# A decoder layer on one core: block 1's output products, norm and first queries placed ahead of blocks 2 and 3, units and branch products over 93 rows, a fourth weight buffer

## The reference

```
z      = x @ W_in            # 9 sections of 1024 columns: q, forget, i, out-gate | conv B, C, h | gate_a, gate_b
o_A    = gated linear recurrence over q, forget, i (8 heads), RMS norm, times silu(out-gate)
o_B    = B * causal_depthwise_conv3(C * h)
mix    = (sigmoid(gate_a) * (o_A @ W_a) + sigmoid(gate_b) * (o_B @ W_b)) @ W_out
x      = LayerNorm(ALPHA * x + mix)
# PEER: per token, 8 heads
qh     = x @ w_q                                    # 8 heads x 2 halves x 128
s1, i1 = top16(qh[:, h, 0] @ keys[h, 0].T);  s2, i2 = top16(qh[:, h, 1] @ keys[h, 1].T)
eidx   = the best 16 of the 256 sums s1 + s2, as i1 * 128 + i2;  g = softmax of these 16
peer   = sum over h, k of g * gelu(u[eidx] . x) * v[eidx]      # u, v: 16384 rows of 1024
x      = LayerNorm(ALPHA * x + peer)
x      = x + sigmoid(x @ W_pg) * (p @ W_pp)
```

## Time and profile before

| | |
|---|---|
| three runs, us | 1784.62 (median), 1783.69, 1786.54 |
| the profiled execution's own time, us | 1783.85 |
| its span, first to last instruction, us | 1781.9 |
| PE busy | 1572.8 us (88%) |
| DVE busy | 1321.1 us (74%) |
| ACT busy | 778.3 us (44%) |
| POOL busy | 497.4 us (28%) |
| moved by DMA | 655.40 MB, of which 536.90 MB by the gathers |
| mean granted TensorE clock | 0.984 |

### The profile page before, as it was taken

How to read it: one execution, slowest core, us unless ns; L and a number is a source line. 1 busy time by engine, 2 the same in 40 slices (tenths; PEclk the granted TensorE clock), 3 DMA queues, 4 the chain that set the end, 5 groups by cost and what they waited for, 6 DMA issues and landing times. The chain is left out here.

```text
span 1781.9 us, 16998 instructions
## 1 busy us (share of the span) xinstructions
PE 1572.8 (88%) x5000; PEld 874.4 (49%) x5000; DVE 1321.1 (74%) x2804; ACT 778.3 (44%) x1937; POOL 497.4 (28%) x528
## 2 busy tenths in 40 slices
PE   8999999999999997989888668788898878787778
PEld 7888888766655575544344223333333323222224
DVE  4454588599888999678878886886666687766666
ACT  6567695422222224343334334444444443444453
POOL 0000000122222232324333443333333333333331
PEclk9999999999999999999999999999999999999999
DMA  5113289799999999999999999999999999999994
GB/s 205 70 70 141 94 317 402 281 421 421 397 419 421 422 406 404 424 417 421 421 415 415 421 421 422 420 422 421 421 421 422 419 408 422 422 419 421 422 410 179
DMA packets 94933, 655.40 MB, mean 368 GB/s; under 512 B 10368, under 2 KB 14208, under 8 KB 17152
## 3 DMA queue, kind: packets, MB, share of 16 engines
q0 software_dynamic: 73728, 536.90, 72.8%
q1 hardware_dynamic: 20832, 116.97, 16.7%
q10 hardware_dynamic: 288, 0.52, 0.1%
HBM read 652.26 MB, written 2.10 MB: 367 GB/s over the span
## 5 line engine op out<-in xcount | busy, mean ns | idle before, releaser
L2111 PE MATMUL psum<-uv,diag 128*128 128x512 f32 x1424 | 707.3, 627 | 193.3 <-ACT diag L991 189.9
L720 POOL DMA_INDIRECT uv<-in_pk_uv,idx x512 | 495.0, 967 | 1249.6 <-PE psum L2111 563.9
L1596 DVE CUSTOM_DVE_ANT_0 uv<-uv,psum 128x1024 f32<-128x1024 f32 x512 | 622.9, 1217 | 295.1 <-DMA uv<-in_pk_uv,idx 288.0
L2111 PEld LDWEIGHTS psum<-uv,diag 128*128 128x128 f32 x1424 | 257.7, 194 | 613.2 <-ACT diag L991 389.7
L979 ACT ACTIVATE gelu<-dots 128x1 f32<-128x1 f32 x512 | 103.5, 202 | 764.1 <-DVE dots L1596 761.9
L2011 PE MATMUL psum<-xT,raw 128*128 128x384 f32 x640 | 208.4, 486 | 0.0
L1609 DVE SCALAR_TENSOR_TENSOR oT<-uv,coef,oT 128x1024 f32<-128x1024 f32 x151 | 193.3, 1280 | 4.2 <-ACT coef L983 4.2
L2011 PEld LDWEIGHTS psum<-xT,raw 128*128 128x128 f32 x640 | 120.7, 190 | 81.7
L983 ACT ACTIVATE coef<-gelu,weight 128x1 f32<-128x1 f32 x512 | 150.8, 295 | 16.6
L991 ACT ACTIVATE diag<-ident,coef 128x128 f32<-128x128 f32 x356 | 143.0, 402 | 11.6
L1847 PE MATMUL psum<-xTh,w_hi 128*128 128x512 f32 x248 | 98.6, 398 | 0.0
(11 more groups left out here) (284 smaller groups left out, 1722.5 us busy)
## 6 DMA issues: line engine op xcount, KB each, us to landing
raw<-in_w_in SPq DMA_DIRECT2D x32, 1024.0 KB, 8.9
raw_a<-in_w_a SPq DMA_DIRECT2D x12, 1024.0 KB, 4.8
raw<-in_pk_w_q SPq DMA_DIRECT2D x10, 1024.0 KB, 9.5
raw_y<-in_w_in SPq DMA_DIRECT2D x8, 1024.0 KB, 6.8
raw<-in_w_branch_a SPq DMA_DIRECT2D x8, 1024.0 KB, 7.7
uv<-in_pk_uv,idx POOLq DMA_INDIRECT x512, 14.6
raw<-in_w_out SPq DMA_DIRECT2D x6, 1024.0 KB, 9.6
raw_w<-in_pk_w_q SPq DMA_DIRECT2D x6, 1024.0 KB, 9.5
```

Source lines behind the costliest of these rows:

```text
L720: pool.indirect_dma_start(row_uv(r)[:], None, pk_uv, bass.IndirectOffsetOnAxis(idx[:, i % 2, j:j + 1], 0)).then_inc(row_loaded(r)[0], 16)
L1596: V.tensor_tensor_reduce(u, u, x_cur[:], 1.0, 0.0, ALU.mult, ALU.add, dots[:, r % 32:r % 32 + 1]).then_inc(dot_done, 1)
L2111: last = T.matmul(B[i][:], diag[:, n % DR, :], row_uv(r)[:, D + i * 512:D + (i + 1) * 512], start=(r in FIRST), stop=last_of_block, skip_g ...
```

## The change

The order of the work beside the rows is rewritten; nothing of what is computed changes.

- Units take rows 0 to 67 (MERGE0 = 68), branch products 68 to 92.
- Output products: the four chunks of block 1 at rows 94 to 98, then blocks 2 and 3 at rows 99 to 112. Norms at rows 101, 115, 117; turns at 104, 118, 120.
- Heads 0 and 1 (SPLIT = 2) are queried for block 1 alone, at rows 106 to 108 and 111 to 113, and for blocks 2 and 3 together at 122 to 125 and 128 to 131; heads 2 to 7 for all three blocks from row 134.
- A thirteenth slot, number 12, in the columns of blocks 2 and 3 of the scores' first half; the loads from unit load 2 to the output chunks go through four slots (RING). Unit load 2 goes to slot 12 and waits for nothing; each later load waits for the load four before it, not three.
- SHARED holds block 0's rows up to 112 and no others of block 0. MERGE_R is 105 (before 91), QUERY_R 212 (211).
- SP loads w_gate behind the fourth of the new query loads and w_ple behind head 1's second query.
- In the final part, block 0 is turned at row 149, its gate products are at 152 to 167, its projection at 169 to 172.

```diff
+            if i == 12:
+                return scores[:, 0, :, 2 * P:]
...
+        SPLIT = 2
+        MERGE0 = 68
...
-        UNIT_ROW += [[(UNIT_MM * n + i) * 58 // (UNIT_MM * (len(UNITS) - EARLY)) for i in range(UNIT_MM)]
+        UNIT_ROW += [[(UNIT_MM * n + i) * MERGE0 // (UNIT_MM * (len(UNITS) - EARLY)) for i in range(UNIT_MM)]
...
-        MERGE_ROW = [58 + n * 23 // 128 for n in range(16 * KT)]
-        OUT_ROW = [83 + n * 11 // 96 for n in range(4 * (TB - 1) * KT)]
-        NORM_ROW = [None] + [OUT_ROW[-1] + 1 + 2 * b for b in range(1, TB)]
+        MERGE_ROW = [MERGE0 + n * 25 // 128 for n in range(16 * KT)]
+        OUT0 = MERGE_ROW[-1] + 2
+        OUTS = [(c, 1) for c in range(4)] + [(c, b) for c in range(4) for b in range(2, TB)]
+        OUT_ROW = [OUT0 + n * 5 // 32 for n in range(4 * KT)]
+        OUT_ROW += [OUT0 + 5 + n * 14 // 64 for n in range(4 * (TB - 2) * KT)]
+        NORM_ROW = [None, OUT0 + 7] + [OUT_ROW[-1] + 3 + 2 * b for b in range(TB - 2)]
...
+        LATER = [(1, h) for h in range(SPLIT)] + [(2, h) for h in range(SPLIT)] + [(1, h) for h in range(SPLIT, PKH)]
+        QUERY0 = {(1, 0): (TURN_ROW[1] + 2, 3), (1, 1): (TURN_ROW[1] + 7, 3), (2, 0): (TURN_ROW[3] + 2, 4),
+                  (2, 1): (TURN_ROW[3] + 8, 4), (1, 2): (TURN_ROW[3] + 14, 6), (1, 3): (TURN_ROW[3] + 22, 7)}
+        QUERY0.update({(1, h): (123 + 14 * (h - 2), 9) for h in range(4, PKH)})
...
-                if r <= OUT_ROW[-1] + 3:
-                    return True
-                return r % 3 == 1 and 106 <= r <= 120
+                return r <= OUT_ROW[-1]
...
-        MERGE_R, QUERY_R = BLOCK_ROWS - 2 - 5 * (UV + 1), QUERY_ROW[-1][-1] + 11
+        MERGE_R, QUERY_R = BLOCK_ROWS - 2 - 3 * (UV + 1), QUERY_ROW[1, PKH - 1][-1] + 11
...
-        FIN_TURN = 5
-        FIN_GATE = [8 + n for n in range(2 * KT)]
+        FIN_TURN = [21] + [5] * (TB - 1)
+        FIN_GATE = [[t + 3 + n for n in range(2 * KT)] for t in FIN_TURN]
...
-        LOADS += [(("unit", n), n - 2 if n < 4 else (n - 2) % 3) for n in range(2, len(UNITS) // 2)]
-        LOADS += [(("merge", m), m % 3) for m in range(8)]
-        LOADS += [(("out", c), (c + 2) % 3) for c in range(4)]
-        LOADS += [(("query", 1, h), h % 2) for h in range(PKH)]
+        RING = (0, 1, 2, 12)
+        LOADS += [(("unit", n), 12 if n == 2 else RING[(n - 3) % 4]) for n in range(2, len(UNITS) // 2)]
+        LOADS += [(("merge", m), RING[(m + 1) % 4]) for m in range(8)]
+        LOADS += [(("out", c), RING[(c + 1) % 4]) for c in range(4)]
+        LOADS += [(("query", 1, h), (1, 2, 0)[h] if h < 3 else h % 2) for h in range(PKH)]
...
             fetch(pk_w_q[2], "query", 0, 2)
-            sp.wait_ge(t_done, USE["unit", 1] + 1)
             unit_fetch(2)
             for h in (3, 4, 5):
                 sp.wait_ge(t_done, USE["query", 0, h - 3, 1] + 1)
                 fetch(pk_w_q[h], "query", 0, h)
+            sp.wait_ge(t_done, USE["unit", 1] + 1)
+            unit_fetch(3)
             sp.wait_ge(t_done, USE["unit", 3] + 1)
-            unit_fetch(3)
+            unit_fetch(4)
...
-            query_fetch(0)
-            query_fetch(1)
-            sp.wait_ge(t_done, chunk_end(11))
-            sp.dma_start(w_ple[:], ple_w_proj).then_inc(ple_in, 16)
-
+            for h in range(4):
+                query_fetch(h)
             sp.wait_ge(x1_done, TB)
             sp.dma_start(w_gate[:], ple_w_gate).then_inc(gate_in, 16)
-            query_fetch(2)
-            query_fetch(3)
+            sp.wait_ge(t_done, query_end(2, 1))
+            sp.dma_start(w_ple[:], ple_w_proj).then_inc(ple_in, 16)
             load_p(0)
```

More of the change, by code:

```diff
@@ L229, in build @@
         first_in = [sem(f"first_in{j}") for j in range(4)]
-        raw_in = [sem(f"raw_in{i}") for i in range(12)]
+        raw_in = [sem(f"raw_in{i}") for i in range(13)]
         consts = sem("consts")
@@ L373, in row_previous @@
             return max((q for q in range(r) if UV_SLOT[q] == UV_SLOT[r]), default=None)
-        FIN_TURN = 5
-        FIN_GATE = [8 + n for n in range(2 * KT)]
-        FIN_P = [FIN_GATE[-1] + 2 + n for n in range(4)]
+        FIN_TURN = [21] + [5] * (TB - 1)
+        FIN_GATE = [[t + 3 + n for n in range(2 * KT)] for t in FIN_TURN]
+        FIN_P = [[rows[-1] + 2 + n for n in range(4)] for rows in FIN_GATE]
         P_BANK = (6, 4)
@@ L433, in blocks, with asked, asked_with @@
             return range(*PIECES[pc])
+        def asked(pc, h):
+            if pc == 1:
+                return range(1, 2 if h < SPLIT else TB)
+            return range(0, 1) if pc == 0 else range(2, TB)
+        def asked_with(i):
+            b, h = divmod(i, PKH)
+            return 0 if b == 0 else 2 if b > 1 and h < SPLIT else 1
         USES, BANK = [], []
@@ L474, in build @@
                     use(UNIT_BANK[n % 4], "unit", n)
[L475 to L482, removed]
+        for n in range(16):
+            use(4 + (n + 2) % 4, "merge", 1, n // 4, n % 4)
+        for r in range(OUT_ROW[0], SCORE_ROW[1, PKH - 1] + 1):
+            for n, (c, b) in enumerate(OUTS):
+                if r == OUT_ROW[KT * n + KT - 1]:
+                    use(4 + (n + 2) % 4 if b == 1 else (0, 1, 6, 7)[n % 4], "out", 1, c, b)
+            for b in range(1, TB):
+                if r == TURN_ROW[b]:
+                    for kh in range(2):
+                        use((4 if b == 1 else 6) + kh, "turn", 1, b, kh)
+            for q in LATER:
+                for a in range(2):
+                    if r == QUERY_ROW[q][KT * a + KT - 1]:
+                        use(4 + a, "query", *q, a)
+                if r == SCORE_ROW[q]:
+                    for a in range(2):
+                        use(4 + a, "query", *q, 2 + a)
         USE = {name: n for n, name in enumerate(USES)}
@@ L529, in chunk_end, with query_end @@
             return USE["out", 1, m - 8, TB - 1] + 1
+        def query_end(pc, h):
+            return USE["query", pc, h, 1] + 1
         @block.sync
@@ L1007, in tail_row @@
                         turn_out(1, b)
-                for h in range(PKH):
+                for q in LATER:
                     for a in range(2):
[L1010 to L1013, removed]
+                        if r == QUERY_ROW[q][KT * a + KT - 1] + 1:
+                            query_out(*q, [a])
+                    if r == SCORE_ROW[q] + 1:
+                        query_out(*q, [2, 3])
             def x2_turn_out(b):
@@ L1453, in search @@
                 if k == 0:
-                    dve.wait_ge(*t_reader(USE["query", min(i // PKH, 1), i % PKH, 3]))
+                    dve.wait_ge(*t_reader(USE["query", asked_with(i), i % PKH, 3]))
                     for a in range(2):
@@ L1741, in tail_row @@
                         merge(1, n // 4, n % 4)
-                for n in range(4 * (TB - 1)):
+                for n, (c, b) in enumerate(OUTS):
                     if r == OUT_ROW[KT * n + KT - 1] + 3:
-                        residual(1, n // (TB - 1), 1 + n % (TB - 1))
+                        residual(1, c, b)
                 for b in range(1, TB):
@@ L2062, in query @@
             def query(pc, h, a, ks=range(KT)):
-                bs = blocks(pc)
-                t = slice(bs[0] * P, (bs[-1] + 1) * P)
+                bs = asked(pc, h)
                 n = P * len(bs)
-                w = slot(SLOT["query", pc, h])
-                turned = x1T0 if pc == 0 else oT[:, :, P:]
+                name = ("query", min(pc, 1), h)
+                w = slot(SLOT[name])
+                turned = x1T0 if pc == 0 else oT[:, :, bs[0] * P:(bs[-1] + 1) * P]
                 r = USE["query", pc, h, a]
@@ L2071, in query @@
                     if k == 0:
-                        pe.wait_ge(*loaded("query", pc, h))
+                        pe.wait_ge(*loaded(*name))
                         if h == 0 and pc > 0:
-                            pe.wait_ge(*t_reader(USE["turn", pc, bs[-1], 1]))
+                            pe.wait_ge(*t_reader(USE["turn", 1, bs[-1], 1]))
                         t_free(r)
@@ L2091, in score @@
                     for i in range(len(bs)):
-                        last = T.matmul(B[bank(r)][:, i * P:(i + 1) * P], qhT[pc][:, a, i * P:(i + 1) * P],
+                        last = T.matmul(B[bank(r)][:, i * P:(i + 1) * P], qhT[pc > 0][:, a, (at + i) * P:(at + i + 1) * P],
                                         keysT[:, 2 * h + a, :], start=True, stop=True, skip_group_check=True)
@@ L2201, in tail_row @@
                         turn_x(1, b)
-                for h in range(PKH):
-                    for n, t in enumerate(QUERY_ROW[h]):
+                for q in LATER:
+                    for n, t in enumerate(QUERY_ROW[q]):
                         if r == t:
-                            query(1, h, n // KT, [n % KT])
-                    if r == SCORE_ROW[h]:
-                        score(1, h)
+                            query(*q, n // KT, [n % KT])
+                    if r == SCORE_ROW[q]:
+                        score(*q)
```

59 lines of the change are left out of this document (29 added, 30 removed).

## The result

The changed kernel takes 1803.99 us (median, 1802.99 to 1808.61), the kernel before 1785.53 us (1783.69 to 1786.54) beside it: ratio 1.0106, 95% interval 1.0093 to 1.0119, so 18.9 us slower (0.0106 of 1784.6, as all ratios below are turned into us; the medians are 18.5 apart). The forecast was 1786.1, with 1792.0 as its upper end. The profiled execution is the slowest of the changed kernel's: own time 1808.61 us, span 1806.6, against 1783.85 and 1781.9 before. Its 24.7 us more are to be explained in the trace. Some 3.3 us of them belong to this one execution and not to the change: it issues its first gather at 340.00 us, while all ten other profiled runs of this document issue theirs at 335.85 to 337.24.

The account below looks back on a forecast made before the run. The DMA pipe, saturated by gathers from about 340 to 1750 us, was taken as the bound. Terms -1.1 - 0.8 + 2.4 + 0 + 1.0 = +1.5 us gave 1785.3, with 0.8 for the median 1786.1; range 1781.0 to 1792.0.

Parts of the forecast that it names:

- The load of w_gate moves from row 108 to about 127, w_ple behind row 131: SP's later weight loads: same bytes, wanted at rows 152 and 169, so cost 0.
- block 0's gate matmuls to rows 152 to 167: Block 0's final part, moved to later rows: same work, cost 0.
- The spread: Units and branch products over 93 rows: TensorE gets cover, DMA idle at 450 and 640 us is won, -1.1 us.
- +11 sums: Block 0's rows 0 to 112 summed on VectorE, 113 in place of 102: 13 us more on it, +1.0 us.
- ring: Fourth weight buffer, slot 12: early unit load -0.8 us, 1 KB packets +2.4 us, slower landings 0.
- early load: Unit load 2 moves into the idle pipe before the first gather: -0.8 us, bounds 0 and 2.5.
- The packets: Slot-12 loads in 1 KB runs, 21 us each: 0.35 us lost a load, +2.4 us for seven, bounds 0 and 4.
- The full stretch of VectorE: Rows 94 to 112, VectorE and pipe about even: idle at 700:720 us stays and as much again, +1.0 us, bounds 0 and 6.
- Slot-12 loads come late: Rival: out load 2 or 3 lands after VectorE needs it at row 101, +4 to +10 us, 1791; chance 0.15.
- VectorE becomes the bound in rows 85 to 112: Rival: 13 us more VectorE work there and one buffer less leave DMA idle, +3 to +6 us, 1790.5; chance 0.15.

Follow-up runs that it names:

- e1: The changed kernel with the ln2_bias load issued ahead of the wait for head 1's second query and of w_ple: 1792.83 us, ratio 1.0046.
- e2: e1 with the w_gate load also moved ahead of head 3's queries: 1787.47 us, ratio 1.0015.
- e4: The kernel before with only the ln2_bias load moved, behind head 4's queries: 1793.68 us, ratio 1.0053.
- e5: e2 with block 0's projection moved later, to rows 174 to 177: 1784.34 us, ratio 1.0003.
- e8: The kernel before with block 0's final part 16 rows later (gate 152 to 167, projection 169 to 172): 1787.97 us, ratio 1.0022.
- e3: The kernel before with only slot 12 and the early unit load added: 1785.45 us, ratio 1.0003.
- e6: e5 with the sums of rows 115, 118, 121 and 124 on VectorE in place of TensorE: 1786.48 us, ratio 1.0014.
- e7: e5 with units back in rows 0 to 57 and branch products in 58 to 80: 1796.93 us, ratio 1.0075.
- e9: e5 without the four-slot ring and early unit load; slot 12 keeps one load, head 3's queries get another slot: 1784.09 us, ratio 0.9998.

## Why the prediction was wrong

In order of size, against +18.9:

- *"The load of w_gate moves from row 108 to about 127, w_ple behind row 131 ...: same bytes, wanted at 152 and 169. Cost 0"*. **This is the step that failed.** It looked up when w_gate and w_ple are wanted and never named what is queued behind them: ln2_bias, 0.5 MB, wanted at row 132. Moving w_ple's wait ahead of it costs 10.7 us (e1), w_gate's late place another 5.5 (e2), together 16.2. e4 gives the same kind of loss, 9.5, by the bias's order alone. Nor did it ask what the pipe does at the place that w_gate leaves: at 755:780 it falls to 345 GB/s in the changed kernel and stays at 425 with w_gate there (e2), which is some 2.5 of the 5.5 us.
- *"block 0's gate matmuls to rows 152 to 167"*, also at cost 0: the projection follows them to 169 to 172, where TensorE is full with head 5's queries. 2.1 us by e5, 3.9 by e8. I had asked only whether the work was the same, not what TensorE does in the new rows.
- The spread, +11 sums, ring and early load, which I had at +1.5 together, measure +0.5 (-1.1 to +2.1, e5). That the sum comes so near is in part luck, as each term was off and the errors cancel; the next four points go by the table of leads, in which two traces differ by about 1 us without a cause.
- The early load: I had -0.8, since I took the gathers' start to leave idle what the load had won. The whole 1.05 MB counts: the pipe is 1.9 to 3.0 us ahead at 345 in e1, e2, e3, e5, e6 and e7. The hole is partly filled (at 320:340 the kernel before moves 171 GB/s, e5 229), and the first gather leaves at 336.61 in e5 (336.66 in the earlier trace rows).
- The packets: the pace was right, 20 us of transfer and landings at 25.1 to 31.9 us, median 26.0, in e5 (21 and 25 in the sum), and small packets rose by 22400 - 14208 = 8192. The price was not: 3.5 us, near the upper bound of 4, not 2.4. I had averaged two windows of some 2.5 us each, too short to show the rate. I had also worked out a price, 1.4 us as an estimate, from the fixed cost of about 3 cycles a packet that the Trainium skill ("DMA: Bandwidth & Descriptors", Why small descriptors are slow) states; the traces show more than twice that, and the measurement decides.
- The spread: I had -1.1. e9, without ring and early load, gains 3.4 us from 345 to 690. I had read the idle pipe by its share; by the rate, against 421 GB/s, has 1.5 us at 450:460 and 1.8 at 640:660; both dips are gone (417 and 422 GB/s after). At 660:670 of the kernel after the share is 1.03 and the rate 403 GB/s; at 710:720 before it is 0.95 and 382, 6% by the share and 9% by the rate. GB/s is the measure of the pipe.
- The full stretch of VectorE behind it: I had +1.0; e5 loses 1.9 us from 690 to 760. The dip at 700 to 720 stayed, as foretold (400 and 361 GB/s against 392 and 382).
- *"Slot-12 loads come late"*: not in the change. Loads to the old slots do get slower (raw<-in_w_in 11.7 us to landing in place of 8.9), yet VectorE is busy 59.64 of 60 us at 640:700. The rival's mechanism is real all the same, as e7 shows (6.6 us).
- *"VectorE becomes the bound in rows 85 to 112"*: 1.9 us in e5, under the 3 to 6 of the rival, and 3.9 in the trace of the changed kernel, 690 to 760 us in both; e6 pays for four sums more. Which part of the 3.9 is the missing w_gate load of 755:780 is not shown.

The chance of a slower kernel was put at 0.30, and no rival named the wait that came. The mechanism that all of it goes through, a pipe that is paid for whenever it stands empty, was right; I didn't apply it to the loads of the norm.

## What to carry to other kernels

When an issue with a wait moves in a queue that runs in order, list every later issue of that queue with its own due time, the smallest ones too: half a megabyte, 13 us late to leave, cost 10.7 us, the place of a load of 4.2 MB 5.5 us. Work moved "to later rows at the same cost" needs a look at how full its engine is in these rows and at who reads the result in order. A large load is also filler: it costs least where the engines that free the buffers are full and the pipe would idle. And where the DMA pipe is the bound, compare the bytes moved up to fixed times: by the end alone the spread, the early load and the small packets looked like nothing, while they moved the pipe by 3.4, 2.5 and 3.5 us.

## What the runs showed of the hardware

```profile
DMA packets 1775, 7.37 MB, mean 410 GB/s; under 512 B 99, under 2 KB 986, under 8 KB 986
...
q0 software_dynamic: 888, 6.46, 87.1%
q1 hardware_dynamic: 887, 0.91, 14.9%
```

  The load of 1.05 MB thus takes 18 us x 1.05 / 0.91 = 20.7 us. Its packets take 14.9% of 16 x 18 us / 887 = 48 ns each. All windows of 20 us in which such a load of e5 runs show this rate:

```profile
386.00:406.00 20.00, 20.00 (x84) 13.26 (x83) 18.32 (x38) 3.57 (x16) 5.62 (x6) 1.00 1.02 411
427.00:447.00 20.00, 20.00 (x87) 13.38 (x86) 19.18 (x39) 4.12 (x18) 5.28 (x7) 1.00 1.02 410
...
658.00:678.00 20.00, 6.73 (x21) 3.88 (x20) 19.93 (x41) 2.98 (x12) 5.62 (x6) 0.78 1.03 412
```

- The same 0.5 MB load lands 7.4 us after its issue (before), 13.5 (after, behind w_ple) and 18.3 (e1, behind w_gate): its time grows with what stands ahead of it in its queue.
